# Computing the first 256 output columns behind five norms from unscaled tokens, in a chain of transformer blocks on one core

## The reference

```python
def rmsnorm(x, g):
    y = x * rsqrt(mean(x * x, axis=-1) + EPS)      # one factor per token
    return y * g                                   # one gain per channel

def ada_norm(x, g, shift, scale):
    return rms_norm(x, g) * (1.0 + scale) + shift  # scale, shift: per channel
```

## Time and profile before

| | |
|---|---|
| time, median of 3 runs | 2181.34 us (2180.09 to 2181.69) |
| the profiled execution's own time | 2176.95 us |
| its span in the profile | 2175.2 us |
| mean granted clock of PE | 0.981 of 2.4 GHz |

### The profile page before, as it was taken

How to read it: one execution, slowest core, us unless ns; L and a number is a source line. 1 busy time by engine, 2 the same in 40 slices (tenths; PEclk the granted TensorE clock), 3 DMA queues, 4 the chain that set the end, 5 groups by cost and what they waited for, 6 DMA issues and landing times. The chain is left out here.

```text
span 2175.2 us, 36150 instructions
## 1 busy us (share of the span) xinstructions
PE 2073.0 (95%) x15028; PEld 1828.1 (84%) x15028; DVE 1253.0 (58%) x1939; ACT 1036.3 (48%) x1896; POOL 33.4 (2%) x32
## 2 busy tenths in 40 slices
PE   7988999999998999999998999989999998999998
PEld 6858989999998999999986876768888887679998
DVE  6776588877887555555574237553333225556554
ACT  5664444467776444444464226443232215555543
POOL 0000000000000000000010000010000001000000
PEclk9989999999999999999998999999999999999999
DMA  6603577754444777777754310122223232114553
GB/s 209 200 1 126 175 261 261 260 177 146 146 141 132 237 265 260 254 260 259 243 175 165 96 59 2 59 78 88 96 88 101 93 97 90 53 41 163 186 190 120
DMA packets 91250, 329.15 MB, mean 151 GB/s; under 512 B 10064, under 2 KB 12496, under 8 KB 90832
## 3 DMA queue, kind: packets, MB, share of 16 engines
q1 hardware_dynamic: 91088, 326.85, 45.4%
HBM read 325.76 MB, written 1.05 MB: 150 GB/s over the span
## 5 line engine op out<-in xcount | busy, mean ns | idle before, releaser
L321 DVE TENSOR_TENSOR wlo<-raw,whi 128x1024 fp32r<-128x1024 f32 (+1 forms) x502 | 614.5, 1226 | 567.5 <-ACT whi L315 564.6
L315 ACT ACTIVATE whi<-raw 128x1024 fp32r<-128x1024 f32 (+1 forms) x502 | 527.0, 1052 | 472.7 <-PE ps L503 428.4
L501 PE MATMUL ps<-x_hi,whi 128*128 128x512 f32 (+1 forms) x1040 | 360.5, 347 | 28.3 <-DVE x_lo L484 23.2
L502 PE MATMUL ps<-x_lo,whi 128*128 128x512 f32 (+1 forms) x1040 | 358.4, 345 | 0.0
L503 PE MATMUL ps<-x_hi,wlo 128*128 128x512 f32 (+1 forms) x1040 | 358.2, 344 | 0.0
L501 PE MATMUL ps<-xT_hi,whi 128*128 128x256 f32 x1152 | 329.6, 286 | 4.1 <-DVE xT_lo L482 4.1
L502 PE MATMUL ps<-xT_lo,whi 128*128 128x256 f32 x1152 | 322.3, 280 | 0.0
L503 PE MATMUL ps<-xT_hi,wlo 128*128 128x256 f32 x1152 | 321.9, 279 | 0.0
L501 PE MATMUL ps<-gh,whi 128*128 128x256 f32 x1024 | 290.4, 284 | 5.6 <-DVE gl L1813 5.6
L502 PE MATMUL ps<-gl,whi 128*128 128x256 f32 x1024 | 286.9, 280 | 0.0
L503 PE MATMUL ps<-gh,wlo 128*128 128x256 f32 x1024 | 286.7, 280 | 0.0
(11 more groups left out here) (354 smaller groups left out, 2965.8 us busy)
## 6 DMA issues: line engine op xcount, KB each, us to landing
raw<-peer_u_t SPq DMA_DIRECT2D x128, 512.0 KB, 3.6
raw<-peer_v_t SPq DMA_DIRECT2D x128, 512.0 KB, 4.4
raw<-ada_t SPq DMA_DIRECT2D x96, 512.0 KB, 5.4
raw<-ffn_in_t SPq DMA_DIRECT2D x88, 512.0 KB, 3.5
raw<-ffn_out_t SPq DMA_DIRECT2D x44, 512.0 KB, 3.8
raw<-qkv_t SPq DMA_DIRECT2D x36, 512.0 KB, 3.5
raw<-w_in_t SPq DMA_DIRECT2D x24, 512.0 KB, 4.3
raw<-peer_wq_t SPq DMA_DIRECT2D x16, 512.0 KB, 3.5
```

Source lines behind the costliest of these rows:

```text
L315: act.activation(whi[:, n % SPLIT, 0:w], raw[:, g % RAW, 0:w], ACT.Copy).then_inc(hi_done, 1)
L321: dve.tensor_tensor(wlo[:, n % SPLIT, 0:w], raw[:, g % RAW, 0:w], whi[:, n % SPLIT, 0:w].bitcast(F32), ALU.subtract).then_inc(lo_done, 1)
L501: pe.matmul(place, wh, xh, start=start, stop=False, skip_group_check=shared)
L502: pe.matmul(place, wh, xl, start=False, stop=False, skip_group_check=shared)
```

## The change

A factor per token commutes with a product over channels. So for the first 256 output columns behind each of the five norms (the two leading column blocks, j = 0 and 1, the "lead") the product is made from `gain * h`, without the token's factor, and the factor is multiplied onto the result. The shift is no part of the token: it rides along as two more columns per half (256 and 257), whose result is a bias for each output channel.

- Weights are laid out anew (`_split_tiles`): two pieces hold columns 0 to 255 of all chunks, the next two columns 256 to 511. In the first qkv stage keys now come ahead of queries.
- In the stage ahead of the norm, ACT and DVE round `gain * h` per column after the square (`Lead.act`, `Lead.dve`). PE runs the lead behind the last column: 2 blocks x 8 chunks x 3 products, in a wide norm twice, for latents and context, 258 columns each (256 without a shift). The sums stand before its chunk 3 (chunk 4 in mix1). Four pieces of the next stage are now split in this stage, and the norm's root, and the scaling and rounding of its first 1 (narrow) or 2 (wide) chunks, are done before the block ends.
- In the next block PE begins with the other two columns (for mix1 with the first query tile). After DVE has made all remaining chunks it copies the bias and multiplies the lead in PSUM (`finish`); then ACT adds the bias on the way out (`out`).
- In `feed_forward` the banks of the tiles are swapped, so tile 1 goes to the banks that held the lead, and PE waits for `act_evacuated.at(2)` ahead of it. The `Rope` matmuls behind the fourth piece move to banks 0 and 1, with the same wait.

The core of the diff:

```diff
+            def pe(self, pe, norm, folds):
+                n = T if self.shifts is None else T + 2
+                for c in range(C):
+                    if c == self.sums_at:
+                        norm.sums(pe, [*range(folds + 1, C - 1), 0, C - 1], folds)
+                    at = pieces[self.first + c // 4][3]
+                    if c % 4 == 0:
+                        pe.wait_ge(lo_done, at + 1)
+                    pe.wait_ge(lead_parted.h, lead_parted.at(self.upto(c)))
+                    for j in range(2):
+                        w = c % 4 * 2 * P + j * P
+                        for s in range(norm.segs):
+                            mm = products(pe, ps[:, norm.segs * j + s, 0:n], [y[:, at % SPLIT, w:w + P] for y in (whi, wlo)],
+                                          [y[:, c, s, 0:n] for y in self.parts], c == 0, c == C - 1)
...
+            def act_end(self, act, norm):
+                g = self.first
+                split_hi(act, g + 2)
+                if norm.n == T:
+                    split_hi(act, g + 3)
+                act.wait_ge(early_sums.h, early_sums.at(1))
+                norm.inverse(act)
+                if norm.n > T:
+                    split_hi(act, g + 3)
+                norm.round(act, 0, self.ready)
+            def dve_end(self, dve, norm):
+                split_lo(dve, self.first + 2)
+                split_lo(dve, self.first + 3)
+                norm.invert(dve)
+                norm.scale(dve, 0, self.ready)
+            def finish(self, dve, norm, j):
+                if self.shifts is not None:
+                    at = ps[:, norm.segs * j:norm.segs * j + norm.segs, T:T + 1]
+                    dve.tensor_copy(lead_bias[:, j, 0:norm.segs].unsqueeze(2), at).then_inc(lead_scaled.h, 1)
+                    place = ps[:, norm.segs * j:norm.segs * j + norm.segs, 0:T]
+                    dve.tensor_tensor(place, place, norm.rstd[:, :].rearrange("p (s t) -> p s t", t=T), ALU.mult).then_inc(lead_scaled.h, 1)
+            def out(self, act, norm, j, dst, kind):
+                act.wait_ge(lead_scaled.h, lead_scaled.at(2 * j + 2))
+                for s, place in enumerate(self.places(norm, j)):
+                    ins = act.activation(dst[:, s * T:s * T + T], place, kind, bias=lead_bias[:, j, s:s + 1])
...
@@ product_stage, ACT @@
-                            if ids[w] >= split_upto[0] and not (before and t == 0):
+                            if ids[w] >= split_upto[0] and (lead or not (before and t == 0)):
                                 split_hi(act, ids[w])
                             if t >= 1 and i == min(1, n_pc - 1):
                                 take_out(t - 1)
...
@@ feed_forward, PE @@
-                    for t in range(TILES):
+                    for t in range(1, TILES):
+                        if t == 1:
+                            pe.wait_ge(act_evacuated.h, act_evacuated.at(2))
...
@@ Rope, PE @@
+                    if w == 3:
+                        pe.wait_ge(act_evacuated.h, act_evacuated.at(2))
                     for n in {3: (0, 1), 7: (2, 3), 10: (4, 5)}.get(w, ()):
                         pe.wait_ge(gq_squared, n + 1)
-                        pe.matmul(ps[:, 4 + n % 2, :], k("ones64"), sq[:, n, :], start=True, stop=True).then_inc(gq_sum, 1)
+                        pe.matmul(ps[:, n % 2, :], k("ones64"), sq[:, n, :], start=True, stop=True).then_inc(gq_sum, 1)
```

More of the change, by code:

```diff
@@ L422, in end_early, with inverse @@
                 early_sums.advance(1)
+                if self.lead:
+                    self.lead.end()
+            def inverse(self, act):
+                act.activation(self.root[:, :], ps[:, self.bank, 0:self.n], ACT.Ln if self.logs else ACT.Sqrt,
+                               bias=eps[:, :], scale=1.0 / D).then_inc(self.root_done.h, 1)
+                if self.logs:
+                    act.wait_ge(self.root_done.h, self.root_done.at(1))
+                    act.activation(self.rstd[:, :], self.root[:, :], ACT.Exp, scale=-0.5).then_inc(self.rstd_done.h, 1)
@@ new lines, in round @@
+            def round(self, act, a, b, before=None):
+                for c in range(a, b):
+                    if before:
+                        before(c)
+                    act.wait_ge(self.scaled.h, self.scaled.at(c + 1))
+                    for s in range(self.segs):
+                        t = self.segment(s)
+                        kind, add = (ACT.Copy, {}) if self.shift is None else (ACT.Identity, {"bias": self.shift(c, s)})
+                        ins = act.activation(self.parts[0][:, c, t], self.x[:, c, t], kind, **add)
+                    ins.then_inc(self.rounded.h, 1)
@@ L433, in act @@
-                if self.logs:
-                    act.wait_ge(root_done.h, root_done.at(1))
-                    act.activation(self.rstd[:, :], self.root[:, :], ACT.Exp, scale=-0.5).then_inc(rstd_done.h, 1)
-                if self.parts:
[L437 to L444, removed]
+                if not self.lead:
+                    self.inverse(act)
@@ L525, in product_stage @@
                 at += n_pc
-            after = ahead(ids[-1] + 1)
+            after = list(range(then.lead.first, then.lead.first + then.lead.more)) if then else ahead(ids[-1] + 1)
+            lead = before.lead if before else None
+            START = 4 if lead else 0
             END = min(2, tiles[-1][0]) if then else 0
@@ L552, in product_stage @@
             with ExitStack() as own, nc.Block() as block:
-                if before:
+                if before and not lead:
                     before.buffers(own)
+                if then:
+                    then.buffers(own)
                 @block.sync
@@ L559, in _ @@
                         sync(sp)
-                    loads(sp, ids[-1] + 1 + RAW)
+                    loads(sp, ids[-1] + 1 + RAW + (len(after) if then else 0))
                 @block.tensor
@@ L624, in _ @@
                                 mm.then_inc(column_done.h, 1)
-                        then.sums(pe, [*range(FOLDS + 1, C - 1), 0, C - 1], FOLDS)
+                        then.lead.pe(pe, then, FOLDS)
                 if then:
@@ L685, in take_out @@
                         for j, job in enumerate(tiles[t][3]):
+                            if lead and t == 0:
+                                lead.finish(dve, before, j)
+                                if job[4] is not None:
+                                    job[4](dve, lead.places(before, j)[0]).then_inc(dve_evacuated.h, 1)
+                                continue
                             if then and t == LAST and j < len(tiles[t][3]) - 1:
@@ L2108, in feed_forward @@
             FOLDS = 3 if w == T else 5
-            after = ahead(g2 + FC)
+            lead = norm.lead
             with ExitStack() as own, nc.Block() as block:
@@ L2112, in feed_forward @@
                 tmp = own.enter_context(nc.sbuf_tensor(f"ffn_tmp{i}", [P, 4, w], F32))
-                norm.buffers(own)
-                def of_first(c):
-                    return [g1 + c // 2] if c % 2 == 0 and g1 + c // 2 >= split_upto[0] else []
+                then = then(hid)
+                if then.lead:
+                    then.buffers(own)
+                after = list(range(then.lead.first, then.lead.first + then.lead.more)) if then.lead else []
                 def bank(t, j):
-                    return ps[:, 4 * (t % 2) + j, 0:w]
+                    return ps[:, 4 * ((t + 1) % 2) + j, 0:w]
                 @block.sync
                 def _(sp):
-                    loads(sp, g2 + FC + RAW)
+                    loads(sp, g2 + FC + RAW + len(after))
                 @block.tensor
```

330 lines of the change are left out of this document (236 added, 94 removed).

## The result

| | time, median (runs) | ratio to before, 95% interval |
|---|---|---|
| before | 2180.09 us (2176.22 to 2182.62, 11) | 1 |
| the changed kernel | 2187.41 us (2184.31 to 2192.79, 11) | 1.0037 [1.0026, 1.0048] |

The account below looks back on a forecast made before the run. PE, busy 95%, was taken as the bound, with 40.6 us to win from idling and low clock. Gains of 3.8 less 4.3 for clock falls gave -0.5, carried to the median 2181.34 + 0.5: 2182 us, range 2172 to 2190.

Parts of the forecast that it names:

- mix1: Norm ahead of the second qkv stage: a new 7.7 us wait before `gqa_squares`, a loss of 3.0 us before clock falls.
- five chains: Step-by-step timings of PE, ACT and DVE at the five norms: together 3.8 us gained if the clock never falls.
- mix0: Norm ahead of the first qkv stage: a gain of 6.0 us before clock falls, with a new wait of 3.1.
- ffn0: Norm ahead of the first feed-forward: a gain of 2.8 us, with PE idling 2.0 instead of 5.9, then 2.6.
- wq: Norm before `peer_wq`: a gain of 0.2 us before clock falls.
- ffn1: Norm ahead of the second feed-forward, narrow: a loss of 2.2 us before clock falls.
- first waits: PE's waits behind the leads, released by the end of a block: 2.0 to 3.5 us, their clock fall hidden.
- second waits: PE's later waits for ACT's take-out or DVE's split: 1.5 to 7.7 us, clock falls priced at 4.3 in all.
- old losses of 11.1 us: Time lost to low clock in the windows behind the five norms before the change, 1.7 to 3.0 us each.
- Work is the same as before: Pricing step: the lead takes PE 11.3 us where the same columns took 11.1 (wide), 5.6 and 5.6 (narrow).
- Rival 2: Slower: every second wait drops the clock for as long as before, 11.1 us against 3.8, +7.3, 2189; chance 0.30.
- Rival 1: Waits shrink and the clock stays: 2176, chance 0.16; stronger form 2169, chance 0.06; full prize 2141, chance 0.02.

Follow-up runs that it names:

- run 1: The changed kernel with operand tiles put back at the earlier kernel's places, 32 bytes past a multiple of 128, no instruction changed: 2180.1 us, ratio 0.9999.
- experiment 5: The changed kernel with only `xT_hi` and `xT_lo` moved from 96 to 32 bytes past a multiple of 128: 2177.85 us, ratio 1.0003.
- experiment 8: 32 unused bytes ahead of `h2`: in the kernel before, 2170.96 us (0.9958); in the kernel with only wq, mix0, ffn0 leads and earlier places, 2169.16 us (0.9946).

## Why the prediction was right, and where it failed

The measured 2187.4 us lies inside the range by luck: what moves it away from the forecast 2182 is a term that the prediction did not have.

**What held.** The five chains, in their sum. With the places equal the change gives 0.9999, where the sum gave -0.5 us of 2181. By place, the gain less the clock's share as forecast: mix0 +5.2 (measured +4.2), ffn0 +2.0 (+3.0), wq +0.2 (+1.0), mix1 -4.7 (-4.3), ffn1 -3.1 (-3.6). The first waits of 2.0, 2.4, 3.5, 3.3, 3.1 (ffn0, mix0, mix1, ffn1, wq) were 1.4, 3.3, 2.9, 3.1, 3.0, released by the ends of blocks as said. The largest second wait is at `gqa_squares`, behind ACT's take-out, 5.4 to 6.5 where 7.7 was forecast.

**Errors that cancelled.** The total of the five places is right by more than its terms deserve. The waits came out smaller than forecast: `finish` was taken at 0.8 us, and the multiply in PSUM took 0.69, one `finish` following the other after 0.66; the second waits were 1.9 against 2.6 (ffn0), 2.1 against 2.9 (ffn1), 0.8 in run 1 against 3.1 (mix0), none against 1.5 (wq). In run 1 the waits at the five norms add up to 25.6 us. The prediction named a total far from 32 as a sign that it was wrong, and this total is well under it.

The clock came out worse. I let the old losses of 11.1 us go and put 4.3 in their place. The same reading (length x (1 - PEclk), from PE's first matmul behind a wait) in run 1, for wq, mix0, both waits of mix1, both of ffn1:

```profile
212.61:225.00 12.39, 12.39 (x82) 12.27 (x83) 9.97 (x20) 6.94 (x12) 0.00 (x0) 0.76 0.25 87
1165.37:1179.34 13.97, 13.97 (x48) 10.80 (x48) 11.69 (x29) 8.47 (x18) 0.00 (x0) 0.80 0.73 300
1825.91:1833.30 7.39, 7.38 (x48) 7.19 (x48) 7.20 (x18) 4.17 (x10) 0.00 (x0) 0.77 0.17 45
1839.84:1850.00 10.16, 10.16 (x61) 8.11 (x62) 4.85 (x5) 9.51 (x12) 0.00 (x0) 0.83 0.45 156
1979.80:1987.45 7.65, 7.57 (x48) 7.07 (x48) 7.29 (x19) 5.44 (x10) 0.00 (x0) 0.78 0.05 18
1989.56:2000.00 10.44, 10.44 (x76) 10.44 (x77) 4.88 (x7) 3.94 (x6) 0.00 (x0) 0.84 0.54 187
```

That is 3.0 + 2.8 + 1.7 + 1.7 + 1.7 + 1.7 = 12.6 us, and none at ffn0. So the forecast had the clock 8.3 us too good and the waits some 6.5 too bad, and the two cancelled. At mix0 the waits are 1.3 under the forecast, the clock's loss is 2.8 where 0.9 was put, and the gain is a microsecond less.

**What failed.** The step "Work is the same as before" under Prices. It took every matmul at what it cost before, outside the five places too, so that they cancelled. In the changed kernel some 6,500 matmuls on `xT`, `gh` and `gl` cost 0.001 to 0.003 us more each, and some 2,100 wide ones mostly 0.0045 less. Run 1 shows it as the whole of the loss. No forecast or rival had this term, and nothing in the list of what would show the prediction wrong names it.

**Rival 2** came out at 2189, near the measured 2187.4, and is refuted nevertheless. Its clock was right, with 12.6 us of loss where there were 11.1 before. Its sum was not, because it took the waits at the forecast length: with the places equal the change costs nothing, where the rival's price was 7.3. At ffn0, 1.4 and 1.9 us of wait bring no fall at all (PEclk 1.00 in run 1); first waits of 2.9 to 3.4 in the four other places each have a fall behind them, which I had counted as hidden. The even odds that I gave to second waits between 2.54 and 4.1 us were never tried, since no second wait of run 1 has such a length; one shorter than 2.54, ffn1's of 2.1, has a fall behind it (PEclk 0.84 in 1989.56:2000.00 above), against what I had read from the wait of 2.54. The rule of the Trainium skill that I set beside this rival (TensorE: Matmul & The Clock Gate, HAM oscillation) bears on mix1 and ffn1, where the trace of run 1 agrees (a fall behind each of two waits), and not on ffn0, where it shows none.

**Rival 1** wanted smaller waits and a kept clock. The first half came, 23.4 us against 32 (25.6 in run 1); the second did not.

**Left open.** The windows of the traces give more per place than the executions do (mix1: 4.3 against 1.1 with 3 of uncertainty). One cause may be in stages that none of this touches: in the attention behind mix0 the profile of the kernel without mix1's lead has PEclk 0.69 in 1293:1304 and 0.81 in 1385:1394, run 1's has 1.00 in both, up to 5 us of difference. In its last stretch, 2020:2070, the kernel without mix1's lead also runs 426 matmuls of 256 columns where run 1 runs 431, with the tiles at 32 in both. With one profile a kernel I can't say whether such differences are chance.

## What to carry to other kernels

When a change adds a tensor, however small, look at where every later tile starts before you explain a difference of under 1%: compare the number of matmuls in the same window of an untouched stretch, in more than one profile, since one place can show two paces. Try an unused pad of 32 bytes as a change of its own; here it gave more than the rewrite of five norms. A shorter wait ahead of PE is worth its length only if the clock does not fall there, since the work that now fills the wait runs at half pace.

## What the runs showed of the hardware

I had not expected any of this. The time of an fp32r matmul with a weight load of its own goes with where its operand tile starts in SBUF. The usual paces are, for 256 columns, 0.1167, 0.1178, 0.1200, 0.119 us at 32, 64, 96, 0 bytes past a multiple of 128, for 512 columns 0.233, 0.229, 0.233, 0.232. The order is not the same for both widths. Single stretches run at another pace of this list with the tile where it was (512 columns at 64 in 0.233, 256 columns at 32 in 0.1178). `xT` alone was moved by itself (experiment 5); the pad of experiment 8 moves every tile from `h2` on. A whole kernel moves by 1.15% with 64 unused bytes. Why is not shown: the runs varied the start of the tiles and nothing else, with `whi` and `wlo` at 0 throughout.

The Trainium skill (SBUF — State Buffer, Operand start alignment) asks only that an operand starts at a multiple of its element size, and says that the rule is about legality, not speed. All places here are legal, and the runs add the speed. Its figure for matmuls of 512 columns back to back (TensorE: Matmul & The Clock Gate, Step-by-step: what each phase is for) is 216 ns, with no word of the place; the traces have 229 to 233 for this kernel's fp32r matmuls, each with a weight load of its own, and the measurement decides.
